# Whole fp32 products at the entry of four FFNs, a scanned forget sum, and an odd mask and odd squares that change their place

## The reference, cut to what matters

```
x = x + 0.5 * rmsnorm(swiglu(rmsnorm(x, g[0]), w_ffn_in[l,0], w_ffn_out[l,0]), g[1])
x = x + rmsnorm(mixer(rmsnorm(x, g[2])), g[3])
x = x + 0.5 * rmsnorm(swiglu(rmsnorm(x, g[4]), w_ffn_in[l,1], w_ffn_out[l,1]), g[5])

swiglu(x, w_in, w_out):  g, u = split(x @ w_in, 2);  return (silu(g) * u) @ w_out
even:  c = cumsum(log_sigmoid(f_logit + b_f)) over the tokens;  s = q k^T + c_q - c_k, causal;  p = softmax(s) v
odd:   s = q k^T for two 64-wide maps, masked where chunk(q) < chunk(k), chunks of 64
       a = softmax(s_1) - lam * softmax(s_2);  o = rmsnorm(a v, g) * (1 - lam_init), per head
```

## Time and profile before

| | |
|---|---|
| three runs, median | 2557.03 us (2553.33 to 2557.09) |
| profiled execution | 2557.7 us, its span 2555.5 us, granted clock 0.983 |
| busy share of the span | PE 95%, DVE 66%, ACT 47%, POOL 5% |
| read from HBM | 249.11 MB, 102 GB/s over the span |

### The profile page before, as it was taken

One profiled execution on the slowest core, in us unless ns is written; L12 is line 12 of the kernel. 1 busy time (PEld: TensorE's weight loads), 2 busy tenths in 40 slices (PEclk: granted clock), 3 DMA queues, 4 the chain that ended last, 5 costly groups with the idle time before them and its releaser, 6 DMA issues.

```text
span 2555.5 us, 37705 instructions
## 1 busy us (share of the span) xinstructions
PE 2424.2 (95%) x13907; PEld 2172.0 (85%) x13907; DVE 1694.6 (66%) x2817; ACT 1207.7 (47%) x2243; POOL 121.7 (5%) x177
## 2 busy tenths in 40 slices
PE   6999999999999899999989999999989798999998
PEld 6999987987777899987789998787777577999887
DVE  7777647666666877755687775563236868777546
ACT  5554435344445555434555553453224755545444
POOL 1000001100002000001100000110000010000000
PEclk8999999999999999999999999999997999999999
DMA  5233335421303223334423333343244042333335
GB/s 144 80 88 83 105 126 164 114 72 52 109 24 122 70 83 83 90 125 132 158 73 83 83 88 127 132 149 118 88 124 116 9 140 67 83 91 92 108 128 177
DMA packets 259139, 261.89 MB, mean 102 GB/s; under 512 B 25567, under 2 KB 213999, under 8 KB 258976
## 3 DMA queue, kind: packets, MB, share of 16 engines
q1 hardware_dynamic: 254224, 243.83, 31.9%
q0 software_dynamic: 4464, 14.80, 1.7%
q10 hardware_dynamic: 288, 1.10, 0.1%
HBM read 249.11 MB, written 10.58 MB: 102 GB/s over the span
## 4 chain that ended last, share of the span: by engine, by line
PE 79%; DVE 13%; ACT 3%; issue 3%; DMA 1%; POOL 1%; SPq 0%; DVEq 0%; ACTq 0%; POOLq 0%
PE ps L933 13%; PE ps L935 13%; PE ps L934 13%; PE ps L991 5%; PE ps L992 5%; PE ps L993 5%; PE ps L1420 3%; PE ps L1422 3%; PE ps L1421 3%; PE ps L1050 2%; PE ps L1052 2%; PE ps L1051 2%; DVE w_all L611 1%; DVE xb L733 1%; DVE small L2033 1%
## 5 line engine op out<-in xcount | busy, mean ns | idle before, releaser
L933 PE MATMUL ps<-xb,w_all 128*128 128x320 f32 x2320 | 722.2, 311 | 24.0 <-DVE arena L702 11.2
L934 PE MATMUL ps<-xb,w_all 128*128 128x320 f32 x2320 | 720.0, 310 | 0.0
L935 PE MATMUL ps<-xb,w_all 128*128 128x320 f32 x2320 | 719.9, 310 | 0.0
L933 PEld LDWEIGHTS ps<-xb,w_all 128*128 128x128 f32 x2320 | 438.8, 189 | 29.4 <-DVE w_all L611 16.9
L511 DVE TENSOR_TENSOR w_all<-raw,w_all 128x1024 fp32r<-128x1024 f32 (+1 forms) x204 | 208.1, 1020 | 364.2 <-ACT w_all L521 196.9
L934 PEld LDWEIGHTS ps<-xb,w_all 128*128 128x128 f32 x2320 | 438.6, 189 | 0.0
L935 PEld LDWEIGHTS ps<-xb,w_all 128*128 128x128 f32 x2320 | 438.3, 189 | 0.0
L505 ACT ACTIVATE w_all<-raw 128x1024 fp32r<-128x1024 f32 (+1 forms) x204 | 182.5, 895 | 442.2 <-PE ps L993 237.5
L611 DVE TENSOR_TENSOR w_all<-raw,w_all 128x512 fp32r<-128x512 f32 x404 | 278.1, 690 | 150.6 <-ACT w_all L604 149.8
L604 ACT ACTIVATE w_all<-raw 128x512 fp32r<-128x512 f32 x404 | 253.6, 629 | 197.4 <-PE ps L935 134.8
L991 PE MATMUL ps<-w_all 128*128 128x512 f32 x528 | 205.9, 390 | 0.9 <-DVE w_all L526 0.9
(11 more groups left out here) (375 smaller groups left out, 4075.2 us busy)
## 6 DMA issues: line engine op xcount, KB each, us to landing
raw<-in_w_ffn_out SPq DMA_DIRECT2D x176, 512.0 KB, 3.3
raw<-in_w_ffn_in SPq DMA_DIRECT2D x120, 512.0 KB, 5.1
gain<-in_w_ffn_in SPq DMA_DIRECT2D x56, 512.0 KB, 4.3
raw<-in_w_in_odd SPq DMA_DIRECT2D x56, 256.0 KB, 2.7
raw<-in_w_out_even SPq DMA_DIRECT2D x16, 512.0 KB, 3.4
raw<-in_w_out_odd SPq DMA_DIRECT2D x16, 512.0 KB, 3.5
gain<-in_norm_g POOLq DMA_DIRECT2D x12, 512.0 KB, 6.3
raw<-in_w_in_even SPq DMA_DIRECT2D x24, 256.0 KB, 2.7
```

Source lines behind the costliest of these rows:

```text
L933: nc.tensor.matmul(dst, wl, xh[:, k, :], start=fresh and k == 0, stop=False, skip_group_check=True)
L934: nc.tensor.matmul(dst, wh, xl[:, k, :], start=False, stop=False, skip_group_check=True)
L935: mm = nc.tensor.matmul(dst, wh, xh[:, k, :], start=False, stop=(k == HK - 1), skip_group_check=True)
```

## The change

It has four parts. (a) In each FFN the 14 products of the first two pairs (`WHOLE = 2`) are made as whole fp32 matmuls, four per product in place of twelve, from the raw weights and unsplit token operands. Their operands are neither rounded nor subtracted; the T's are written to a place of their own, so that the splits of the token side come later (`X_FRONT`), the sequence begins in another order, the transposes of tiles 3 and 4 stand together ahead of P2 of pair 1, and raw buffers of the first pairs wait for the product in place of the split. (b) For the even layer log-forget is transposed by four matmuls, one DVE scan over 512 elements makes the running sums of all heads (`c_rows`), four transposes bring them back for `cq`, and `sums` is one matmul of 512 columns per head. (c) In the odd layer the mask is written to PSUM once (`dve_hidden`), and PE leaves the corner of 64 x 64 alone: two matmuls of w - 64 columns and two of 64 columns for the lower 64 queries per step. The addition at L2031 goes. (d) The odd squares and their sums go from ACT to POOL (`pool_squares`), but for two heads of the last tile.

```
-SEQUENCE = [("P1", 0), ("P1", 1), ("P2", 0), ("P2", 1), ("P1", 2), ("P2", 2)]
-SEQUENCE += [(name, j) for name in ("P5", "P6", "P7", "P4", "P3") for j in range(2)]
+SEQUENCE = [("P1", 0), ("P2", 0), ("P1", 1), ("P2", 1), ("P5", 0), ("P1", 2), ("P6", 0), ("P2", 2), ("P7", 0), ("P5", 1)]
+SEQUENCE += [("P4", 0), ("P6", 1), ("P3", 0), ("P7", 1), ("P5", 2), ("P4", 1), ("P6", 2), ("P3", 1), ("P7", 2)]
...
             elif prev is not None and ffn_of(prev) is not None:
...
+                if i in SPLIT_NO:
+                    sp.wait_ge(op_lo, split_count(f, i))
+                else:
+                    sp.wait_ge(prod_mm, NPROD * f + i + 1)
...
         def dve_xb(dve, f, name):
+
+            if name in T_NO:
+                dve.wait_ge(prod_mm, done_of(f, {x: p for p, x in XOF.items()}[name], WHOLE - 1))
...
-        X_FRONT = {8: "T2", 10: "T3", 12: "T4", 14: "B22"}
+        X_FRONT = {14: "T1", 16: "T2", 18: "T3", 20: "T4", 21: "B22"}
...
+                if j < WHOLE:
+                    w = whole_s2(j) if name == "P6" else operand_raw(f, name, j)
                     for k in range(HK):
+                        mm = nc.tensor.matmul(dst, w[:, k * P:(k + 1) * P], x_whole(XOF[name])[:, k, :],
+                                              start=fresh and k == 0, stop=(k == HK - 1), skip_group_check=True)
...
+        def dve_hidden(dve):
+
+            dve.wait_ge(kt_done, 2 * NS)
+            cols = ps[0:CHUNK, 0:4, :].rearrange("p b (t n) -> p b t n", n=P)[:, :, :, CHUNK:P]
+            for b in range(4):
+                mask = nc.vector.tensor_copy(cols[:, b], con[0:CHUNK, C_NC + CHUNK:C_NC + P].unsqueeze(1)
+                                             .to_broadcast([CHUNK, NP, P - CHUNK]))
+            mask.then_inc(hidden, 1)
...
+                if odd and s == NS - 1:
+                    dve_hidden(dve)
                 normalize(s)
...
-                for kb in range(NP):
-                    for b in range(kb + 1):
-                        mm = nc.tensor.matmul(bank(6, P, kb * P), lgn[:, b, h:h + 1].to_broadcast([P, P]),
-                                              con[:, C_UT:C_UT + P] if b == kb else ones,
-                                              start=(b == 0), stop=(b == kb))
-                mm.then_inc(nc_mm, 1)
+                nc.tensor.matmul(bank(6), con[0:NH, C_ID + h:C_ID + h + 1].to_broadcast([NH, P]), c_rows,
+                                 start=True, stop=True).then_inc(nc_mm, 1)
...
                         for m in range(2):
-                            mm = nc.tensor.matmul(bank(sc_bank(n, odd) + m, w), qTO[64 * m:64 * m + 64, h, i * P:(i + 1) * P],
-                                                  kTO[64 * m:64 * m + 64, h, 0:w], start=True, stop=True)
+                            nc.tensor.matmul(bank(sc_bank(n, odd) + m, w - CHUNK), qTO[64 * m:64 * m + 64, h, i * P:(i + 1) * P],
+                                             kTO[64 * m:64 * m + 64, h, 0:w - CHUNK], start=True, stop=True)
+                        for m in range(2):
+                            mm = nc.tensor.matmul(ps[CHUNK:P, sc_bank(n, odd) + m, w - CHUNK:w],
+                                                  qTO[64 * m:64 * m + 64, h, i * P + CHUNK:(i + 1) * P],
+                                                  kTO[64 * m:64 * m + 64, h, w - CHUNK:w], start=True, stop=True)
...
+            sq = scratch[:, 0:heads * P].rearrange("p (h d) -> p h d", d=P)
+            mine = tok[:, t, 0:heads * P].rearrange("p (h d) -> p h d", d=P)
+            pool_link(pool, nc.gpsimd.tensor_tensor(sq, mine, mine, ALU.mult))
+            w = P // 2
+            while w > 1:
+                pool_link(pool, nc.gpsimd.tensor_tensor(sq[:, :, 0:w], sq[:, :, 0:w], sq[:, :, w:2 * w], ALU.add))
+                w //= 2
...
         def pe_cumulate(pe):
             pe.wait_ge(logf_done, 1)
             for i in range(NP):
-                for b in range(i + 1):
-                    mm = nc.tensor.matmul(bank(7, NH, 64 + i * NH), con[:, C_UT:C_UT + P] if b == i else ones,
-                                          lgf[:, b, :], start=(b == 0), stop=(b == i))
+                mm = nc.tensor.transpose(ps[0:NH, 7, i * P:(i + 1) * P], lgn[:, i, :], ident)
+            mm.then_inc(lg_ps, 1)
...
+                    nc.vector.tensor_tensor_scan(c_rows, con[0:NH, C_ONE:C_ONE + 1].to_broadcast([NH, SEQ]),
+                                                 ps[0:NH, 7, :], 0.0, ALU.mult, ALU.add).then_inc(cum_done, 1)
```

More of the change, by code:

```diff
@@ L130 @@
 PLACE = {key: i for i, key in enumerate(SEQUENCE)}
+WHOLE = 2
+SPLIT = [i for i, (_, j) in enumerate(SEQUENCE) if j >= WHOLE]
+SPLIT_NO = {i: n for n, i in enumerate(SPLIT)}
+NSPLIT = len(SPLIT)
 RING, AHEAD = 5, 4
@@ L169, in build_trunk @@
         xb = at_byte("xb", 14 * BLOCK, [P, 14, HK, HT], F32R)
+        xb_f32 = at_byte("xb_f32", 0, [P, 14, HK, HT], back=14 * BLOCK)
         xT_hi = at_byte("xT_hi", 0, [P, KD, TOK], F32R, back=14 * BLOCK)
@@ L178, in build_trunk @@
         att = at_byte("att", 0, [P, 3456], back=4 * (W_ALL - 4 * BW))
+        w_f32 = at_byte("w_f32", 0, [P, W_ALL], back=4 * W_ALL)
         gain = at_byte("gain", 8 * D, [P, 2, D])
@@ L306, in build_trunk @@
         sq_done, srs_done = sem("sq_done"), sem("srs_done")
+        hidden = sem("hidden")
         block = ctx.enter_context(nc.Block())
@@ L1138, in act_norm_rest @@
             f = FFN_PRE.get("pre%d" % (p + 1))
-            if f is not None:
-                for i in range(2):
-                    act_operand(act, f, i)
-            elif nxt:
+            if nxt:
                 for i in range(2):
@@ L1146, in act_norm_rest @@
             sq_m(act, p, 4)
-            if f is not None:
-                for i in range(2, AHEAD):
-                    act_operand(act, f, i)
             if p == 5:
@@ L1164, in act_norm_start @@
                 sq_x(act, -1, t)
-            act_operand(act, 0, 0)
             for t in TILES[0]:
                 act_xt(act, "pre0", t, t)
-            act_xb_first(act, -1)
-            for i in range(1, AHEAD):
-                act_operand(act, 0, i)
             for t in TILES[1]:
                 sq_x(act, -1, t)
+            act_xb_first(act, -1)
             act.wait_ge(lam_sum, 1)
@@ L1243, in dve_norm_rest @@
             f = FFN_PRE.get("pre%d" % (p + 1))
-            if f is not None:
-                for i in range(2):
-                    dve_operand(dve, f, i)
-            elif nxt:
+            if nxt:
                 for i in range(2):
@@ L1252, in dve_norm_rest @@
             post_gain(dve, p, 4)
-            if f is not None:
-                dve_operand(dve, f, 2)
             if f is None and nxt:
@@ L1259, in dve_norm_rest @@
                 return
-            if f is not None:
-                dve_operand(dve, f, 3)
             pre(dve, p, 3)
@@ L1276, in dve_norm_start @@
                 pre(dve, -1, t)
-            dve_operand(dve, 0, 0)
-            dve_xb_first(dve, -1)
-            for i in range(1, AHEAD):
-                dve_operand(dve, 0, i)
             dve.wait_ge(par_in, 16 * 9)
@@ L1287, in dve_norm_start @@
                 pre(dve, -1, t)
+            dve_xb_first(dve, -1)
+            dve_first_sums(dve, 0, 0)
             dve.wait_ge(wf_hi_done, 1)
@@ L2097, in norm_row, with pool_link, pool_squares @@
             return t % 2 if t < NP else 2
+        LAST_HEADS = 2
+        def pool_link(pool, ins):
+            pool_count[0] += 1
+            ins.then_inc(gs, 1)
+            pool.wait_ge(gs, pool_count[0])
+        def pool_squares(pool, t):
+            heads = NH - LAST_HEADS if t == NP - 1 else NH
+            if t < NP:
+                pool.wait_ge(o_done, NSTEP + t * NH + heads)
+            else:
+                pool.wait_ge(sot_done, 2)
+            sq = scratch[:, 0:heads * P].rearrange("p (h d) -> p h d", d=P)
[5 more added lines that the diff above has]
+                w //= 2
+            last = nc.gpsimd.tensor_tensor(s_ss[:, norm_row(t), 0:heads].unsqueeze(2), sq[:, :, 0:1], sq[:, :, 1:2], ALU.add)
+            pool_link(pool, last)
         def act_square_head(act, t, h):
             row = norm_row(t)
-            if t < NP:
-                act.wait_ge(o_done, NSTEP + t * NH + h + 1)
-                if t >= 2 and h == 0:
-                    act.wait_ge(srs_done, t)
-            at0 = (h if t < NP else (h + 4) % NH) * P
+            act.wait_ge(o_done, NSTEP + t * NH + h + 1)
+            at0 = h * P
             sq = nc.scalar.activation(scratch[:, at0:at0 + P], tok[:, t, h * P:(h + 1) * P], ACT.Square,
```

200 lines of the change are left out of this document (111 added, 89 removed).

## The result

| | before | changed |
|---|---|---|
| median of six runs | 2555.31 us (2553.33 to 2557.09) | 2565.16 us (2561.77 to 2567.16) |
| ratio | | 1.0036, 95% interval 1.0024 to 1.0047 |
| profiled execution, its span | 2557.7 us, 2555.5 us | 2561.77 us, 2559.9 us |
| granted clock over the span | 0.983 | 0.971 |

The account below looks back on a forecast made before the run. PE, busy 95% of the span, was taken as the bound, with FFN entries and odd attention bound by DVE. Entries -30.1, even sums -10.5, projection 0 and odd attention 0 gave -41 us: 2516 us median, range 2503 to 2540.

Parts of the forecast that it names:

- Even forget sums: Even attention: one 512-column matmul for ten saves 1.47 us in each of 8 heads; -10.5 us taken, bounds -4.4 and -11.8.
- R3: Rival, FFN entries: whole products run at the low clock, 4.4 us each; all 56 cost +123 us, 2639; chance 0.05.
- Entries: First 20 products of the four FFN entries: whole products gain 30.1 us together, bounds -15 and -34.
- 45.1: Entries f = 1 to 3: forecast time in us for the first 20 products, from 53.4, 52.2 and 52.4.
- the other lists: Entries: token splits, the refilled third buffer and PSUM-freeing results, checked and said to come 0.3 to 2 us ahead of PE.
- R2: Rival, FFN entries: a new wait takes 3.8 of each entry's 7.5 us, +15, 2531; chance 0.13.
- Odd attention: Odd layer: mask -7.4, copies +1.4, PE matmuls +1, POOL contention +5; sum 0 us, bounds -6 and +17.
- The mask's saving: Odd attention: the mask leaves DVE's chain, 0.21 + 0.02 us a step over 32 steps, -7.4 us.
- Projection: Even projection: transposes and a 1.2 us scan replace 2.15 us of PE; zero, bounds -1 and +1.
- R1: Rival, odd attention: POOL's squares block DVE's combinations, 4 us x 5 tiles = 20 us, 2536; chance 0.13.
- the sentence with +15: Odd attention: by the skill's shared-port rule for DVE and GpSimd, the odd sum comes to +15 us in place of 0.
- R4: Rival, even attention: DVE or ACT takes over the head at 8 to 8.5 us, about +7 us, 2523; chance 0.12.

Follow-up runs that it names:

- e2: Changed kernel with the scanned sums in a 128-row tile, 120 rows zeros, one 128-row matmul of 512 columns a head: 2538.35 us, ratio 0.9935.
- e6: Changed kernel with the sums as one 128-row matmul of 512 columns (120 rows zeros), made twice over per head: 2525.69 us, ratio 0.9887.
- e3: Kernel before with the scanned sums alone (transposes, scan, one 8-row matmul per head): 2591.3 us, ratio 1.014.
- e5: Changed kernel with the odd mask added on DVE step by step again and two score matmuls a step: 2569.42 us, one run.
- e10: Changed kernel with 128-row sums made twice, odd squares on ACT, and added 128-row matmuls in odd query blocks 0 and 1: 2526.44 us, ratio 0.9886.
- e4: Changed kernel with the odd squares on ACT again, as before the change: 2563.55 us, one run.
- e7: Changed kernel with the 8-row sums matmul of each head made three times over: 2593.75 us, one run.

## Why the prediction was wrong, step by step

**The step that failed is "Even forget sums".** It took 1.47 us off each head, "on an engine that never idles there", and kept the price of everything else in the head: -10.5. Measured were +31.9 in the even stretch. The saving was right at the upper clock: a late head of e2 took 7.66 us for the 7.53 of the sum, and the changed kernel's own second head, still at 1.00, took 7.45 (8.42 before). What the step left out is that the work removed had a part in keeping the clock there. Removed were 160 matmul records over 128 rows; what remained per head were scores over 64 rows, transposes and 64-column products over 128, and a matmul over 8 rows, and with that mix the clock fell to 0.50. PE paces the heads, so all its work was slowed: from the sums of the third head to the output projection it took 94.8 us for 62.3, at 14.2 us a head for 9.0.

**The rival R3 had the low clock, in the wrong place and from another cause.** It looked for it at the entries, where PE waits, and priced it at twice the duration. It came in the even attention, with PE busy throughout, and a head took nearly twice as long (14.2 us for 7.6). The 0.06 for a slower kernel stood for the most part on R3, so on another cause than the one that came. The row it was dismissed by, 1.00 in the even attention, was a row of work that the change itself took away. A clock read from the kernel before holds for the work that was there.

The Trainium skill (TensorE: Matmul & The Clock Gate, "What's actually happening") describes the half-rate clock as the state of an engine that isn't busy, which activity ends. Here the trace differs: by its records PE was busy 14.20 of 14.20 us, head after head, at 0.50. These runs show which work was there when the clock fell and rose; what the chip itself looks at they don't show. In e2 and e6 the rows of both operands of the matmul were raised together, so which of the two counts stays open.

**Entries: right, a little less than forecast.** 25.6 us for 30.1. A whole product has a pitch of 2.15 us, the prediction's lower bound, for the 2.2 interpolated, and P2_1 starts at 9.2 to 9.5 us for the 9.9 of the chain. The 0.9 to 1.2 us by which 45.1 was passed in f = 1 to 3 are less than one wait: P7_2 stands 1.3 to 1.5 us for ACT (L707), which itself waited for DVE's multiplication at L751, queued behind a split of the token side (L777) and more. In f = 1:

```profile
884.39 0.38 PE L974 MATMUL ps<-xb,w_all 128*128 128x320 f32 x1 [1.31 <-ACT scratch L707]
883.80 0.44 ACT L707 ACTIVATE scratch<-ps 128x320 f32<-128x320 f32 x1 [1.80 <-DVE arena L751]
```

That the other lists ran "0.3 to 2 us ahead of PE" was wrong at this one product, whose PSUM bank the prediction hadn't listed. The first entry lost 2.0 us there, 1.1 at P7_0 and 1.3 at P5_0, and the 5 us that the forecast had set down for the low clock weren't needed, since the clock was 1.00; that its 21st product came at 66.7 for 65.3 us is in part luck. R2, the larger form of such a wait, did not come.

**Odd attention: the sum right, its terms not all.** Forecast 0, measured +1.0, which is no more than traces with the same odd code differ by (147.14 and 145.91 us in before and e3). The mask's saving was counted as 32 equal steps, -7.4; the blocks gained 3.5 against e5, half of what was counted, since PE paces the early steps at the low clock, and the later start took most of that. POOL's collisions were taken at 5; DVE's combinations grew by 2.6, and the move of the squares cost 2.5 in all, half of that behind the last maximum, where the clock falls. `dve_hidden` took 1.39 us for 1.4. POOL's squares of 1024 elements took 1.89 us, 1.85 ns an element, between the bounds of 0.95 and 2.9.

**Projection:** zero forecast, 2.7 gained, partly by the entry's end; nothing hung on it.

**Two slips of arithmetic.** The four terms of the sum give -40.6, so 2517.1 for the profiled execution and not 2516.8. R1's 2536 adds its 20 us to a sum that has 5 for the same collisions already; by the prediction's own terms it is 2531, as in the sentence with +15. Neither changes the account.

R4 can't be judged at this clock in the changed kernel; in e6 a head comes to 8.5 us because PE works 8.5, so neither DVE nor ACT took over. The head with 8.3 us of DVE's work ran in no trace at both the upper clock and one matmul for its sums, so for that head R4 stays open.

## What to carry to other kernels

Where PE sets the pace, ask of each matmul that a change removes not only how long it took but what it did for the granted clock: matmuls over 128 rows that look wasteful were here what kept the rest of the stage at the upper level. Read the clock by windows of the size of a step on both sides of a change, before any busy share: a stage with fewer records and more busy time has changed its clock. And a stretch found at the lower level with PE busy throughout is worth a try with added matmuls over all 128 rows, as in e6 and e10; in e10 they also took back part of what they gave.

## What was not expected of the hardware

A matmul over 8 rows and one over 128 rows, of which 120 are zeros, made the same sums, but with the first the even attention stayed at 0.50 from its second or third head on in every trace (changed, e3, e4, e5, e7) and with the second the clock came back in mid-stage. Matmuls whose result is written over made a kernel 13 us faster. And the clock's return isn't certain: runs of the kernel with one wide matmul a head lay 15 us apart, those with two 7 and those with ten 5.
